# Four key picks placed between weight splits, and half of the output weights split in the last attention duo

## The reference: what is computed

```python
z = x @ w_in                       # one projection for all three branches
o_diff = diff_attention(...)       # branch "d" here: softmax minus lam * softmax
o_dsa  = dsa_attention(...)        # branch "s": only the 128 best keys of a query count
o_fox  = forgetting_attention(...) # branch "f": causal, with a decay
y = gates[0]*(o_diff @ w_br[0]) + gates[1]*(o_dsa @ w_br[1]) + gates[2]*(o_fox @ w_br[2])
m = y @ w_o
h = layer_norm(ALPHA * h + m);  f = grouped_moe(h, ...);  h = layer_norm(ALPHA * h + f)
```

## Time and profile before

| | |
|---|---|
| median of 3 runs | 2232.84 us (2230.6 to 2236.11) |
| the profiled execution, its own time | 2234.41 us |
| its span, first to last instruction | 2232.7 us |
| PE busy | 2014.1 us, 90% |
| DVE busy | 959.1 us, 43% |
| ACT busy | 672.4 us, 30% |
| mean granted TensorE clock | 0.969 of full |

### The profile page before, as it was taken

The page is one execution under the profiler, slowest core; times in us unless marked ns, Lnnn a source line. Parts: engine busy times, 40 slices in busy tenths (PEclk is TensorE's granted clock), DMA queues, the critical chain, the costliest instruction groups (busy, mean ns, idle before and its releaser), DMA issues.

```text
span 2232.7 us, 30445 instructions
## 1 busy us (share of the span) xinstructions
PE 2014.1 (90%) x10004; PEld 1229.4 (55%) x10012; DVE 959.1 (43%) x1898; ACT 672.4 (30%) x1358; POOL 211.2 (9%) x244
## 2 busy tenths in 40 slices
PE   6999989999979988788999999999998899887887
PEld 5777867877743323222376777778777333222232
DVE  5756855755651111010256666657556311110113
ACT  3544545544310000000144546546551000000000
POOL 3000002000011111111000000110001111111100
PEclk9999999999989998999999999999999899999998
DMA  5321321313589999999942123112138899999996
GB/s 172 114 76 39 114 76 39 113 70 120 232 321 421 425 424 427 425 425 421 389 150 76 39 76 114 39 60 102 67 137 316 338 425 425 425 425 426 426 419 268
DMA packets 104200, 535.63 MB, mean 240 GB/s; under 512 B 14800, under 2 KB 17744, under 8 KB 83552
## 3 DMA queue, kind: packets, MB, share of 16 engines
q1 hardware_dynamic: 92064, 510.41, 57.0%
q0 software_dynamic: 11968, 23.11, 2.8%
HBM read 527.17 MB, written 23.07 MB: 246 GB/s over the span
## 4 chain that ended last, share of the span: by engine, by line
PE 74%; DMA 8%; DVE 7%; issue 5%; ACT 2%; another core or an unknown queue 2%; SPq 1%; DVEq 0%; POOL 0%; ACTq 0%; POOLq 0%
PE ps L1186 17%; PE ps L832 12%; PE ps L834 12%; PE ps L833 12%; PE ps L1206 8%; DMA wslot<-in_w_up 4%; PE ps L951 2%; DMA scr<-in_w_up 2%; PE ps L981 2%; PE ps L1012 2%; PE ps L1176 1%; DMA h<-h_rows 1%; DVE scr L2285 1%; PE ps L1304 1%
## 5 line engine op out<-in xcount | busy, mean ns | idle before, releaser
L2265 DVE COPY scr<-ps 128x512 f32<-128x512 f32 x64 | 44.3, 692 | 726.8 <-PE ps L1176 726.7
L832 PE MATMUL ps<-hT_lo,w_hi 128*128 128x512 f32 (+1 forms) x816 | 327.5, 401 | 7.4 <-DVE w_lo L1721 7.4
L834 PE MATMUL ps<-hT_hi,w_hi 128*128 128x512 f32 (+1 forms) x816 | 319.0, 391 | 0.0
L833 PE MATMUL ps<-hT_hi,w_lo 128*128 128x512 f32 (+1 forms) x816 | 318.2, 390 | 0.0
L1369 ACT ACTIVATE scr<-ps 128x512 f32<-128x512 f32 (+1 forms) x214 | 111.2, 524 | 555.8 <-PE ps L1206 311.4
L1187 PE MATMUL ps<-scr 128*64 128x512 f32 x480 | 231.7, 639 | 0.0
L1206 PE MATMUL ps<-ring,scr 128*64 128x512 f32 x736 | 169.8, 604 | 34.1 <-DVE scr L2285 32.6
L1721 DVE TENSOR_TENSOR w_lo<-ring,w_hi 128x1024 fp32r<-128x1024 f32 x114 | 139.5, 1223 | 119.1 <-ACT w_hi L1389 113.5
L1657 ACT ACTIVATE scr<-ps 64x512 f32<-64x512 f32 x64 | 37.7, 589 | 505.7 <-PE ps L1187 505.7
L1389 ACT ACTIVATE w_hi<-ring 128x1024 fp32r<-128x1024 f32 x114 | 120.3, 1055 | 190.9 <-PE ps L834 162.3
L832 PEld LDWEIGHTS ps<-hT_lo,w_hi 128*128 128x128 f32 (+1 forms) x816 | 153.5, 188 | 40.7 <-issue 9.6
(11 more groups left out here) (269 smaller groups left out, 3348.4 us busy)
## 6 DMA issues: line engine op xcount, KB each, us to landing
ring<-in_w_down SPq DMA_DIRECT2D x42, 2048.0 KB, 46.6
ring<-in_w_in SPq DMA_DIRECT2D x30, 2048.0 KB, 8.1
scr<-in_w_up SPq DMA_DIRECT2D x26, 2048.0 KB, 50.8
xslot<-in_w_up SPq DMA_DIRECT2D x14, 2048.0 KB, 42.9
spare<-in_w_gate SPq DMA_DIRECT2D x14, 2048.0 KB, 46.8
ring<-in_w_gate SPq DMA_DIRECT2D x12, 2048.0 KB, 42.9
scr<-in_w_gate SPq DMA_DIRECT2D x12, 2048.0 KB, 44.3
h<-in_w_gate SPq DMA_DIRECT2D x12, 2048.0 KB, 45.6
```

Of the source, the lines that this page charges most:

```text
L832: mm(out, a[0], b[1], start=first, stop=False)
L833: mm(out, a[1], b[0], start=False, stop=False)
L834: return mm(out, a[0], b[0], start=False, stop=last)
```

## The change

On DVE, the loop of branches d and s splits the units v2, v3, g0-0 and g0-1 one by one; in branch d one pick stands ahead of each, so that picks 36 to 39 are interleaved with the four splits and no longer follow them. For branch s the order is what it was. On ACT and DVE the eight slices of the first half of w_o are rounded and subtracted in turn 8 of branch s, six in its first part and two behind, and no longer in `output_parts` and `last_sum`. The second half of w_o stays where it was. No instruction is added or dropped, and PE's list is the same.

```diff
@@ ACT, attention
                             if m < NDUO:
                                 exps(now[part])
+                            if br == "s" and m == NDUO:
+                                for k in ((0, 1, 2, 3, 4, 5), (6, 7))[part]:
+                                    round_weight(0, k, l)
@@ ACT, output_parts
-                    round_weight(0, 0)
                     for c in range(KD):
                         act.wait_ge(y_summed.sem, y_summed.at(c, l))
                         nc.scalar.activation(y_hi[:, c], by_tile(y_sum), ACT.Copy).then_inc(
                             y_rounded.sem, y_rounded.tick(c))
-                        if c + 1 < KD:
-                            round_weight(0, c + 1)
-                        round_weight(1, c)
+                        round_weight(1, c, l)
@@ DVE, attention
                             if part == 0 and br != "d" and 1 <= m < NDUO + 1:
                                 take_probs(before[0])
+                            if part == 0 and br == "s" and m == NDUO:
+                                for k in range(6):
+                                    low_weight(0, k, l)
...
                             for n in done if br == "d" else done[1:]:
                                 low_heads(n)
+                        if br == "s" and m == NDUO:
+                            for k in (6, 7):
+                                low_weight(0, k, l)
@@ DVE, last_sum
                         V.tensor_tensor(by_tile(y_sum), yT[:, c], by_tile(last_prod), ALU.add).then_inc(
                             y_summed.sem, y_summed.tick(c))
-                        low_weight(0, c)
-
                         dve.wait_ge(y_summed.sem, y_summed.now(l))
@@ DVE, the loop over branches
-                            split_to((br_ + "g0", 1), l)
-                            if br_ == "d":
-                                pick_keys(l, 36, 40)
+                            for n, unit in enumerate(((br_ + "v", 2), (br_ + "v", 3), (br_ + "g0", 0), (br_ + "g0", 1))):
+                                if br_ == "d":
+                                    pick_keys(l, 36 + n, 37 + n)
+                                split_to(unit, l)
```

More of the change, by code:

```diff
@@ L1569, in gates, with round_weight @@
                             split_to(units[min(first + KD + c // 2, len(units) - 1)], l)
-                def output_parts(l):
[L1573 to L1577, removed]
-                    round_weight(0, 0)
+                def round_weight(half, k, l):
+                    name = f"wo{half}"
+                    act.wait_ge(land[in_slot[name]].sem, land[in_slot[name]].at(name, l))
+                    nc.scalar.activation(wo_hi(half, k), wo_raw(half, k), ACT.Copy).then_inc(
+                        wo_rounded.sem, wo_rounded.tick((half, k)))
+                def output_parts(l):
                     for c in range(KD):
@@ L1997, in attention, with low_weight @@
                             pick_keys(l, 12 + m, 13 + m)
+                def low_weight(half, k, l):
+                    dve.wait_ge(wo_rounded.sem, wo_rounded.at((half, k), l))
+                    V.tensor_tensor(wo_lo(half, k), wo_raw(half, k), wo_hi(half, k).bitcast(F32),
+                                    ALU.subtract).then_inc(wo_ready.sem, wo_ready.tick((half, k)))
                 def last_sum(br, l):
@@ L2004, in low @@
                                         ALU.subtract).then_inc(y_ready.sem, y_ready.tick(("y", c)))
[L2006 to L2009, removed]
                     for c in range(KD):
@@ L2026, in last_sum @@
                     for k in range(KD):
-                        low_weight(1, k)
+                        low_weight(1, k, l)
                 def gated_sum(br, l):
```

## The result

| | before | after |
|---|---|---|
| median, same chip (4 runs each) | 2233.65 us | 2214.65 us (2214.03 to 2218.28) |
| ratio, with its 95% interval | | 0.9919 (0.9902 to 0.9936) |
| second comparison, another chip (7 and 4 runs) | 2235.26 us | 2212.12 us (2210.66 to 2218.68) |
| ratio, with its 95% interval | | 0.9902 (0.9884 to 0.9920) |
| the profiled execution, its span | 2232.7 us | 2216.5 us |

The kernel became faster by 0.8 to 1.0%; 2212 was forecast. The profiled execution of after (2218.28 us) was the longest of its four, so the two spans differ by 16.2 us and the medians by 19.0.

What follows compares the result with a forecast made beforehand. The mixer was taken as PE-bound, with PE waiting on ACT and DVE, and the expert stage as DMA-bound once running. Terms of 13.5 and 7.0 us made 20.5 us off, so 2212 us, range 2205 to 2221.

Steps and rivals of the forecast that it cites:

- Term 1: Branch d: picks between splits remove PE's 4.87 us wait and its slow clock, 7.0 and 6.5 us in the two layers.
- the 2.0 us to spare: Branch d: with row maxima 6.9 us earlier, the exponentials are ready 2.0 us before PE asks for them.
- Term 2: Output stage: moving the output weights starts the sums earlier and speeds their pace to 2.15 us a block, 3.5 us per layer.
- two bounds: Pace of the sums without the weight part: 1.92 us a block by DVE alone, 2.18 over ACT; the longer decides.
- The cost of the moved weights: Last turn of branch s: six roundings and low parts fit DVE's 4.35 us idle time, so moving them costs nothing.
- The clock behind the output waits: Output product: remaining waits of about 0.1, 1.6 and 1.5 us are nearly as long, so PE's clock falls again.
- bound of 4.4 us: Output product: upper limit of the gain per layer from moving the weights, cut from 4.9 by PE's own arrival.
- The length of the fall: After the output waits: clock at 0.50 from 579 to 585 us; full clock would save 2.4 us.
- The rival of a clock that stays up: After the output waits the clock does not fall: 2.4 us more per layer, 2207.5 us, chance 0.17.
- Does it reach the end: Expert stage: its steady DMA stream starts when PE arrives, so gains pass through; rival of no change, 2233 us, chance 0.05.
- only the picks pay: Rival: the sums keep their pace or PE meets another wait, so 2219 us, chance 0.13.
- a late weight piece: Rival: a rounding waiting for `wo0` holds up branch s's last turn, 2240 us or more, chance 0.04.

Runs made afterwards that it cites:

- e1: Kernel before with only the four picks moved between the splits, output weights left where they were: 2222.37 us, ratio 0.9944.
- e3: Changed kernel with three picks among the splits and the fourth behind the last split: 2214.85 us in one execution.
- e4: Kernel before with five extra unread products on PE filling its 4.87 us wait before the scores of duo 1 in branch d: 2235.16 us in one execution.
- e5: Changed kernel with the gate's product written to two buffers in turn, so DVE need not wait for its own sum: 2212.14 us in one execution.
- e8: Changed kernel with all eight slices of w_o's first half ahead of the copy of the last probabilities, not six: 2212.24 us in one execution.
- e6: Changed kernel with ACT rounding the first three sums among the sigmoids and w_o's second-half slices rounded two blocks later: 2206.26 us, ratio 0.9876.
- e10: The changed kernel itself measured again, beside e9 on one chip: 2212.12 us, ratio 0.9902.
- e7: Changed kernel with one extra unread product on PE ahead of each of blocks 6 and 7 of the output product: 2210.84 us, ratio 0.9898.
- e9: Changed kernel with the edits of e5 and e6 together: 2206.07 us, ratio 0.9868.
- e2: Kernel before with only the output weights moved into branch s's last turn, picks still behind the splits: 2227.38 us, ratio 0.9966.

## Why the prediction was right, and where its sizes were off

- **Term 1, 13.5 us.** Measured 7.06 + 6.52 = 13.6 between the traces, and some 12.5 in the total of e1. Its working holds step by step: the delayed split ran from 280.58 to 281.80, and PE did not wait for it; the picks fell into ACT's time; the row maxima had at least 1.8 of the 2.0 us to spare (e3); turn 1 took 8.79 us where 8.75 was worked out; and that the clock and not only the wait is in the term is shown by e4.
- **Term 2, 3.5 us a layer.** The mechanism was right and its size was off: 3.04. The start was met (sum 1 stood 6.34 us behind the last quarter in the working and 6.36 in the trace), and so were the 1.46 us to the last low part. The step that failed is the pace: "For the pace without the weight part there are two bounds", DVE alone at 1.92 and the way over ACT at 2.18. The bound by DVE was taken by removing 0.61 us from the old block, but the removed instruction had stood between the sum and the next product, and that product may overwrite its buffer only when the sum has read it. The wait was in the kernel before too, covered by the instruction that left. With it DVE takes 0.90 + 0.61 + 0.72 = 2.23 us a block, and e5, which removes it, shows the way over ACT next at 2.12. Six blocks by 0.07 us are the 0.4 that were missing.
- **The cost of the moved weights, nothing.** Right, with more to spare than was claimed: even the copy that e8 makes 0.7 us later costs PE nothing, by the 18 matmuls that were named as cover. e8 had one execution.
- **The clock behind the output waits.** The forecast was that it falls again, and it did in 8 of 10 layers seen, but its premise came true by luck. The working lets waits of "about 0.1, 1.6 and 1.5 us" remain. Its own times don't give them: with PE at block 7 by 577.4 and able to go on at 578.35, one wait of about 1 us would be left, and behind one wait of 0.95 us (e6) the clock fell in neither layer. What remained is 1.28 + 1.24 us, because PE came to these blocks 1.3 us earlier, counted from the last quarter: 18.51 us (570.03) to block 6, where it was 19.84 (576.69, the 575.99 plus 0.7). The wait of 1.08 us, which the working had missed, was gone with the weight parts. So the bound of 4.4 us "by PE's own arrival" was too low as well.
- **The length of the fall.** It was taken as given by the waits, and e3 and e10 show that it varies from 0 to 6.8 us with the same waits; in time that is 55.9 to 58.7 us to the transposes, 2.8 us a layer. The rival of a clock that stays up (2207.5) was therefore no other case but an end of the same one. What went with a clock that stays up is shorter waits: in the six layers of e6, e7 and e9 it never fell. The rule of the Trainium skill that was weighed ("TensorE: Matmul & The Clock Gate", section "Part 1: The HAM clock gate": one long gap between bursts throttles again) does not describe these traces; here two gaps of 1.28 and 1.24 us were followed by a fall most of the time. The same section of the Trainium skill also tells of another kernel whose frequent short idle times make the clock go up and down, and that is nearer to what the traces show.
- **Does it reach the end.** Yes: the DMA share at the start of the expert stage is 0.67 and then 1.03, where the earlier trace rows have 0.66 and 1.02 in windows that lie ten microseconds later; the transposes of layer one come 7.3 us earlier. From the transposes of layer one (L826) to the scores of duo 0 in layer two it is 1385.83 - 610.26 = 775.6 us, and was 1392.70 - 617.58 = 775.1.
- **The other rivals.** That only the picks pay is refuted by e2 (0.9966, interval below 1), and a late weight piece by the first rounding, which waited for nothing. The sum of 20.5 us was 1.5 more than what the first comparison showed and less than the 23 of the second.

## What to carry to other kernels

An instruction between a producer and its consumer on the same engine hides that engine's wait for itself. Before subtracting an instruction's length from a loop's pace, list which waits it had covered. Put work that has no deadline (here the picks) into the gaps of a strictly ordered engine, ahead of instructions that wait for somebody else anyway; and where PE has a wait that lets its clock fall, the gain is the wait and the slow stretch behind it. Follow PE from wait to wait over the whole stretch that a change touches, other queues' releases of its banks included: here one wait of 1.08 us was left out, and with it PE's arrival was wrong.

## What the runs showed of the hardware that was not expected

- The same pair of PE waits was followed by 0, 3.6 or 6.8 us at the lower clock, by the execution. By the 2.8 us a layer of the table, a comparison of two single executions of the changed kernel is therefore uncertain by 5.6 us from this place alone in two layers. More comes from elsewhere: PE's work up to the scores of duo 0 in layer one is the same in all twelve traces, and they start anywhere from 291.46 (e2) to 295.77 us (e1).
- VectorE's operations on 128x512 elements last 0.69 us but start 0.61 us apart when nothing is between them; where the second waits for the end of the first the distance is 0.88 to 0.90 us. So such a wait cost 0.3 us, of which the trace shows 0.2 as idle time.
